# A transformer kernel on one Trainium2 core: first modulation as rows in column tiles, gate units in the first head's quarters, two reordered waits

## What is computed

```python
c_act = silu(c)
for i in range(2):                                   # first block
    mod = c_act @ ada_w[i] + ada_b[i]                # 1 x 2048 @ 2048 x 6144
    shift, scale, gate = split(mod, 3)
    h = rmsnorm(x, norm_g[i]) * (1 + scale) + shift
    y = retention(h) if i == 0 else latent_attention(h)
    x = x + gate * y
x = rmsnorm(x, final_norm_g)
# second block: forgetting + dilated attention, then the expert layer:
# per token 8 heads x 16 chosen of 16384 experts
hdn = gelu(sum(expert_down[e] * xn)); x += sum_e(gate_e * hdn_e * expert_up[e])
out = rmsnorm(x, final_norm_gain)
```

## Time and profile before

| | us |
|---|---|
| three runs | 2998.37, 3003.18, 3003.22 |
| median | 3003.18 |
| the profiled execution, its time | 2998.47 |
| the profiled execution, its span | 2996.7 |
| PE, DVE, ACT, POOL busy | 2888.4, 2077.0, 1113.0, 541.4 |
| moved by DMA | 799.62 MB, mean 267 GB/s |

### The profile page before, as it was taken

The page is one execution under the profiler, slowest core; times in us unless marked ns, Lnnn a source line. Parts: engine busy times, 40 slices in busy tenths (PEclk is TensorE's granted clock), DMA queues, the critical chain, the costliest instruction groups (busy, mean ns, idle before and its releaser), DMA issues.

```text
span 2996.7 us, 41682 instructions
## 1 busy us (share of the span) xinstructions
PE 2888.4 (96%) x16537; PEld 2414.1 (81%) x16537; DVE 2077.0 (69%) x3117; ACT 1113.0 (37%) x1729; POOL 541.4 (18%) x524
## 2 busy tenths in 40 slices
PE   7999999999999999999999999999999989999998
PEld 7999999998878977798987899888889977444443
DVE  5778777778775455754556658995568999666666
ACT  1344444444445444544445542012026977000000
POOL 0000000000000000000000002333446457544443
PEclk9899999999999999999999999999999999999999
DMA  9977777777866644466443545999998888999998
GB/s 329 355 236 266 267 265 267 268 264 259 295 212 188 173 117 136 147 182 186 126 123 127 192 157 194 338 323 402 395 345 287 292 290 302 404 409 409 409 409 325
DMA packets 359297, 799.62 MB, mean 267 GB/s; under 512 B 40152, under 2 KB 99920, under 8 KB 358336
## 3 DMA queue, kind: packets, MB, share of 16 engines
q1 hardware_dynamic: 284480, 506.28, 49.8%
q0 software_dynamic: 74624, 290.69, 26.3%
HBM read 794.76 MB, written 2.10 MB: 266 GB/s over the span
## 4 chain that ended last, share of the span: by engine, by line
PE 70%; DMA 15%; DVE 6%; issue 3%; ACT 3%; POOL 2%; SPq 0%; DVEq 0%; ACTq 0%; POOLq 0%
PE ps L2021 16%; PE ps L2023 15%; PE ps L2022 15%; PE ps L2570 13%; DMA s<-in_up_rows,s 12%; POOL s L717 2%; DVE s L1971 2%; DMA s<-in_down_rows,s 2%; PE ps L2065 1%; DVE s L1952 1%; PE ps L2601 1%; DVE r L1239 1%; PE ps L2645 1%; PE ps L2615 1%; PE ps L2303 1%
## 5 line engine op out<-in xcount | busy, mean ns | idle before, releaser
L2021 PE MATMUL ps<-r,r 128*128 128x256 f32 (+1 forms) x3232 | 1045.3, 323 | 7.1 <-DVE r L1239 5.3
L2023 PE MATMUL ps<-r,r 128*128 128x256 f32 (+1 forms) x3232 | 1027.2, 318 | 0.0
L2022 PE MATMUL ps<-r,r 128*128 128x256 f32 (+1 forms) x3232 | 1026.8, 318 | 0.0
L1239 DVE TENSOR_TENSOR r<-s,r 128x1024 fp32r<-128x1024 f32 (+2 forms) x532 | 640.2, 1211 | 432.3 <-ACT r L732 431.3
L732 ACT CAST r<-s 128x1024 fp32r<-128x1024 f32 (+2 forms) x532 | 548.9, 1039 | 786.5 <-PE ps L2023 721.4
L2021 PEld LDWEIGHTS ps<-r,r 128*128 128x128 f32 x3232 | 621.2, 192 | 57.6 <-issue 13.7
L2022 PEld LDWEIGHTS ps<-r,r 128*128 128x128 f32 x3232 | 621.2, 192 | 43.2 <-issue 5.3
L2023 PEld LDWEIGHTS ps<-r,r 128*128 128x128 f32 x3232 | 620.5, 192 | 40.5
L2696 PE MATMUL ps<-s,big 128*128 128x512 f32 x1024 | 443.2, 596 | 1.5 <-DMA s<-in_up_blocks 1.5
L1971 DVE SCALAR_TENSOR_TENSOR s<-s,s,s 128x1024 f32<-128x1024 f32 x256 | 328.4, 1283 | 165.4 <-DMA s<-in_up_rows,s 163.7
L1952 DVE CUSTOM_DVE_ANT_0 s<-s,s 128x1152 f32<-128x1152 f32 x256 | 345.6, 1352 | 111.7 <-DMA s<-in_down_rows,s 110.1
(11 more groups left out here) (300 smaller groups left out, 2468.6 us busy)
## 6 DMA issues: line engine op xcount, KB each, us to landing
s<-in_ada_w SPq DMA_DIRECT2D x192, 512.0 KB, 5.9
s<-in_ret_w_in SPq DMA_DIRECT2D x128, 512.0 KB, 5.4
s<-in_up_blocks SPq DMA_DIRECT2D x128, 512.0 KB
s<-in_down_blocks SPq DMA_DIRECT2D x128, 448.0 KB
s<-in_w_in SPq DMA_DIRECT2D x96, 512.0 KB, 3.9
s<-in_ret_w_in SPq DMA_DIRECT2D x128, 256.0 KB, 3.9
s<-in_ret_w_out SPq DMA_DIRECT2D x64, 512.0 KB, 5.7
s<-in_mla_w_in SPq DMA_DIRECT2D x48, 512.0 KB, 3.7
```

The costliest lines, as they stand in the source:

```text
L1239: v.tensor_tensor(lo_of(w), raw_of(w), hi_of(w).bitcast(F), ALU.subtract).then_inc(*lo_made.to(w))
L2021: pe.matmul(o, lh, rh, start=start, stop=False, skip_group_check=True)
L2022: pe.matmul(o, lh, rl, start=False, stop=False, skip_group_check=True)
L2023: return pe.matmul(o, ll, rh, start=False, stop=stop, skip_group_check=True)
```

## The change

1. **Modulation as rows.** `first_direct` and `first_sum` call `into_row`: the column of `cact` (or ones), broadcast to 32 columns, is the stationary operand, and the block's 1024 columns move in four pieces of 256, each into its own 32 partitions of bank 7 (four column tiles). ACT copies the 128 x 256 result to `MODROW`, PE transposes it (`first_turn`), and DVE reads every 32nd column as the modulation. `TENSOR_K` has 8 of 16 k's instead of 6.
2. **Layout of the inputs.** `ada_first` and `ret_first` hold the same numbers as the blocks of the first modulation and the 24 units of head 0, rearranged ahead of the launch so that each entry is one piece of 4 KB per partition (before: two of 2 KB, or four of 1 KB for q and k).
3. **Order of the first head.** Each quarter has six units: two `qk`, two `vals`, two `gate` (w = 6q to 6q + 5), with the sixteen blocks of the next quarter behind the first four. `scores(0)` moves ahead of the last two gate units. Normed x is transposed once, ahead of the modulation, and ACT copies it to `XNT0` in SBUF; scaling reads it there. DVE takes the norm ahead of its first block.
4. **Small loads.** The constant table and the nine gain and bias loads go from SP's queue to GpSimd's, behind x.
5. **Latent values.** The wait for the copy of the values moves from the scores of each group to their first reader.
6. **Ones.** The last one-hot of tile 0 is made after down row 251, the coefficients of tile 1 ahead of the first up row, and tile 1's one-hots ahead of up rows 1 to 32.

```diff
+        XNT0 = at(32 * KB, 16, 256)
+        MODROW = at(YG + 5376, 256)
...
         def mod_entry(q, k):
-                cols_ = A["ada_w"][0][k * 128:(k + 1) * 128, 0:2 * D].rearrange("p (s n) -> p s n", s=2)
-                return [(ap.rearrange("p (s n) -> p s n", s=2), cols_[:, :, q * 512:(q + 1) * 512])]
+            return ("mod", 1024, lambda ap: [(ap, A["ada_first"][q, k])], (q, k))
+        def first_unit(w):
+            return ("w", 1024, lambda ap: [(ap, A["ret_first"][w])], None)
...
         for q in range(4):
-                if q < 3:
-                    plan += [mod_entry(q + 1, 4 * i + k) for k in range(4)]
-        cols512(ret_in, 8192)
+            for x in range(6):
+                plan.append(first_unit(6 * q + x))
+                if q < 3 and x < 4:
+                    plan += [mod_entry(q + 1, 4 * x + k) for k in range(4)]
...
-        TENSOR_K = (1, 4, 7, 10, 13, 15)
+        TENSOR_K = (1, 3, 5, 7, 9, 11, 13, 15)
...
-        HOT_AT = [190 + 2 * q for q in range(29)] + [248, 250]
+        HOT_AT = [190 + 2 * q for q in range(29)] + [248, 250, 251]
...
         def scalar(s):
...
-            s.wait_ge(*col_b.at(0))
             s.activation(XN[:, 0, :], X[:, 0, :], ACT.Square, scale=float(D) ** -0.5, accum_out=st[:, 0:1]).then_inc(*sq_a.to("N0"))
...
+            for p in range(8):
+                s.wait_ge(*turned.at(("N0", p)))
+                s.copy(flat(XNT0[:, 2 * p:2 * p + 2, :]), bank_of_pair("N0", p)).then_inc(*xnt_made.to(p))
             for q in range(4):
-                cast(4 * q)
+                s.wait_ge(*summed.at(("first", q)))
+                if q:
+                    s.wait_ge(*mod_turned.at(q - 1))
+                s.copy(MODROW, bank[7][:, 0:256]).then_inc(*mod_copied.to(q))
+                cast(6 * q)
...
         def vector(v):
...
-            entries(4)
-            v.wait_ge(*cols.at("all"))
...
-            v.wait_ge(*col_b.at(0))
             v.tensor_tensor_reduce(XN[:, 1, :], X[:, 1, :], X[:, 1, :], 1.0 / D, 0.0, ALU.mult, ALU.add,
                                    st[:, 1:2]).then_inc(*sq_v.to("N0"))
+            norm("N0", 0)
             entries(9)
-            norm("N0", 0)
+            v.wait_ge(*cols.at("all"))
...
             hidden(1)
-            first_ones(0, 31)
+            coefficients(1)
             add_row(0)
-            coefficients(1)
-            add_row(1)
-            add_row(2)
-            for n in range(3, 256):
+            for n in range(1, 256):
+                if n <= 32:
+                    first_ones(1, n - 1)
                 add_row(n)
-                if n < 35:
-                    first_ones(1, n - 3)
...
         def tensor(pe):
...
+            def into_row(q, column, w, first, last):
+                for m in range(4):
+                    r = pe.matmul(bank[7][32 * m:32 * m + 32, 0:256], column.broadcast_to([128, 32]), w[:, m * 256:(m + 1) * 256],
+                                  start=first, stop=last, skip_group_check=True)
+                return r
...
-                for m in range(8):
-                    r = pe.matmul(bank[6 + q % 2][:, m:m + 1], raws[i % 8][:, m * 128:(m + 1) * 128], cact[:, k:k + 1],
-                                  start=k == TENSOR_K[0] and m == 0, stop=False, skip_group_check=True)
-                r.then_inc(*mod_t.to(i))
+                into_row(q, cact[:, k:k + 1], raws[i % 8], k == TENSOR_K[0], False).then_inc(*mod_t.to(i))
...
+            def first_turn(q):
+                take(6)
+                pe.wait_ge(*mod_copied.at(q))
+                for j in range(2):
+                    r = pe.transpose(bank[6][:, j * 128:(j + 1) * 128], MODROW[:, j * 128:(j + 1) * 128], IDN)
+                r.then_inc(*mod_turned.to(q))
...
-            for k in TENSOR_K[1:]:
+            for k in TENSOR_K[2:5]:
+                first_direct(0, k)
+            for p in range(8):
+                turn("N0", p, XN, normed("N0"))
+            for k in TENSOR_K[5:]:
                 first_direct(0, k)
             first_sum(0)
+            first_turn(0)
             for q in range(4):
+                for x, (f, u) in enumerate((f, u) for f in (qk, vals, gate) for u in (2 * q, 2 * q + 1)):
+                    if q < 3:
+                        for k in TENSOR_K:
+                            if k // 4 == x:
+                                first_direct(q + 1, k)
+                        if x == 4:
+                            first_sum(q + 1)
+                    if q == 3 and x == 4:
+                        scores(0)
+                    f(0, u, 6 * q + x)
+                    if q < 3 and x == 4:
+                        first_turn(q + 1)
...
-                        pe.wait_ge(*vm_copied.at((g, 1)))
...
                     pe.wait_ge(*flip_copied.at(("M", h)))
+                    if h % 4 == 0:
+                        pe.wait_ge(*vm_copied.at((h // 4, 1)))
```

More of the change, by code:

```diff
@@ L810, in scalar @@
                     turn("N0", p, gs, mod[:, 0:16], HT)
-                for x in range(1, 4):
-                    cast(4 * q + x)
-            for x, dst in enumerate((cosR, sinR, cosM, sinM)):
-                s.wait_ge(*angle.at(x))
-                s.activation(dst, RQ[x], ACT.Sin).then_inc(*sines.to(x))
+                for x in range(1, 6):
+                    cast(6 * q + x)
+                    if q == 3 and x == 3:
+                        for a, dst in enumerate((cosR, sinR, cosM, sinM)):
+                            s.wait_ge(*angle.at(a))
+                            s.activation(dst, RQ[a], ACT.Sin).then_inc(*sines.to(a))
             def v_copy(h):
-                w = 15 if h == 0 else 24 * h + 15
+                w = 21 if h == 0 else 24 * h + 15
                 if h == 0:
@@ L1436, in vector @@
             for q in range(4):
-                entries(entry_of[4 * q] + 1 + (2 if q < 3 else 0))
+                entries(entry_of[6 * q])
                 first_modulation(q)
@@ L1500, in vector @@
             qk_rotate(0)
-            for w in range(16, 20):
+            for w in (20, 21):
                 step(w)
             decay(0)
-            for w in range(20, 24):
+            for w in (22, 23):
                 step(w)
@@ L2103, in turn @@
                 r.then_inc(*turned.to((x, p)))
-                free[b] = turn_a.at((x, p)) if p % 2 else turn_v.at((x, p))
+                free[b] = xnt_made.at(p) if x == "N0" else turn_a.at((x, p)) if p % 2 else turn_v.at((x, p))
             def normed(x):
@@ L2736 @@
     every["table"], every["decay"] = table, decay
+    first = every["ada_w"][0][:, 0:2 * D].reshape(16, 128, 2, 4, 512)
+    every["ada_first"] = np.ascontiguousarray(first.transpose(3, 0, 1, 2, 4)).reshape(4, 16, 128, 1024)
+    ret = every["ret_w_in"][0]
+    heads = [np.concatenate([ret[:, 0:256], ret[:, 2048:2304]], axis=1), ret[:, 4096:4608], ret[:, 8192:8704]]
+    every["ret_first"] = np.ascontiguousarray(np.stack(
+        [f[u * 256:(u + 1) * 256].reshape(2, 128, 512).transpose(1, 0, 2) for q in range(4) for f in heads
+         for u in (2 * q, 2 * q + 1)])).reshape(24, 128, 1024)
     rows = every.pop("peer_down_2")[0]
```

110 lines of the change are left out of this document (44 added, 66 removed).

## The result

The changed kernel took 2965.75 us (median of four runs, 2959.61 to 2967.84), the kernel before 3003.2 beside it (median of four, 2998.37 to 3005.46): a ratio of 0.9873 [0.9859, 0.9888], 37.5 us less. The forecast was 2970 (2957 to 2992). The profiled execution is the shortest of its runs, 2959.61 us with a span of 2957.8; against the profiled execution of before (2998.47) it is 38.9 us shorter.

The account below looks back on a forecast made before the run. PE was taken as the bound, with DMA also at its limit early and in the expert stage's last 440 us. 2998.5 - 22 - 7 - 1.5 = 2968.0, plus half of 4.7, gave 2970 us, range 2957 to 2992.

Parts of the forecast that it names:

- The row product: First head's modulation on PE: four column tiles run side by side, so a block takes 0.7 us.
- The landing of the last block: First head: the last modulation block lands at 120.2 us instead of 127.8.
- The packets: First head's transfers: 4 KB pieces raise DMA from 379 to 409 GB/s, -8.1 us, bounds 0 and -8.1.
- From the landing to `values`: First head's end: nine units, last block with sum and turn, scores and waits take 32.4 us.
- Part 1: First head: `values` begins at 152.6 instead of 174.2, -22 us, bounds -9 and -27.
- The latent wait: Latent heads: PE's four stops of 8.1 us before the groups' first scores go; -7 us, bounds -3 and -9.
- The ones: Expert stage: tile 1's loop starts about 5 us earlier, but DMA must bring the rest; -1.5 us, bounds 0 and -5.
- the point of the part: First head's quarters: six units in the time of four, DMA the bound, PE idle some 5 us in each.
- Rival A: First head: tiles run one behind the other, block 1.9 us, Part 1 gives nothing; 2992 us, chance 0.09.
- Rival C: First head: rows one behind the other at a clock of 0.845, `values` 21 us later; 3013 us, chance 0.05.
- rival B: First head: packets bring no more than 379 GB/s and the start gains nothing; 2983 us, chance 0.10.
- (D): Whole kernel: all bounds on the good side, -27, -9 and -5; 2957.5 us, no chance of its own given.

Follow-up runs that it names:

- experiment 4: Changed kernel with each row product as four full-array matmuls, one behind the other, into the same 256 columns: 2970.12 us, ratio 0.989.
- experiment 3: Changed kernel with the first modulation's blocks and head 0's units read in their old layout, pieces of 2 KB and 1 KB: 2972.25 us, ratio 0.9894.
- experiment 7: Changed kernel with ten of a quarter's 16 blocks on PE instead of eight: 2971.35 us, ratio 0.9889.
- 11: Changed kernel with ten of 16 blocks on PE and a needless matmul ahead of blocks 3, 7, 10 and 15 of quarters 1 to 3: 2963.07 us.
- control: The changed kernel once more, with no edit: 2966.97 us, ratio 0.9875.
- experiment 1: Kernel before, with only the wait for the latent values moved to their first reader: 2988.15 us beside 3004.05, ratio 0.9945.
- 2: Kernel before, with only the last one-hot of tile 0 and tile 1's coefficients and one-hots moved as in the change: 3003.2 us beside 3004.05.
- experiment 6: Changed kernel with the table and the nine small loads back on SP's queue between entries 5 and 6: 2963.85 us, ratio 0.986.

## Why the prediction was right, step by step

**The row product (0.7 us side by side).** Right: 0.64. The four tiles run beside each other, their starts 6 to 8 ns apart (215 ns on the full array); serially the same eight records take 1.89, a factor of 2.95. The Trainium skill, TensorE: Matmul & The Clock Gate, Part 3, lists 2.38 for three column tiles; this trace agrees in kind for four tiles of fp32. Of a drain at a mode change, which the Trainium skill, TensorEngine Tiling (Array Packing), Key Properties, warns of, the trace shows little. Here nothing is waited for ahead of the row product:

```profile
124.42 0.39 PE L2021 MATMUL ps<-r,r 128*128 128x512 f32 x1
124.65 0.39 PE L2022 MATMUL ps<-r,r 128*128 128x512 f32 x1
124.97 0.64 PE L2060 MATMUL ps<-s,s 128*32 128x256 f32 x8
125.53 0.39 PE L2020 MATMUL ps<-r,r 128*128 128x256 f32 x1
```

Full-array matmuls of 512 columns start 0.23 us apart, the row product 0.32 behind the last of them: about 0.09 us. The idle times of 0.15 to 0.26 us ahead of other blocks end with a transfer by the profile, and experiment 4, which never changes the mode, has one of 0.23.

**The landing of the last block (120.2).** Right: 121.45, with two errors that cancel. The first unit starts 8 us earlier (41.3; the sum had given the start 5). The packets carry most of their term: experiment 3 puts it at 5.3 to 6.5 us of the whole time, where the sum had 8.1. But the quarters take 31 to 32 us, not 28.2. DMA has its 409 GB/s only outside the slow windows. What SP's queue waits for in the first 160 us of after (total, times, longest):

```profile
SPq L656 <- DVE r L1244: 57.8, 26, 5.9
SPq L656 <- DVE s L1257: 25.2, 25, 2.1
```

SP stands most of the time before a buffer that DVE has not yet freed by a low part; the six windows from 60 to 120 us average 390 GB/s, by which 22 entries of 0.524 MB are 29.6 us. The remaining 1.4 us or so of a quarter I could not place. Experiments 7 and 11 speak against DVE's products as the cause; DVE's order, the stand before the turned modulation, is what lengthens SP's waits at the change of quarters.

**From the landing to `values` (32.4).** Right: 121.45 to 152.74 is 31.3. Part 1 together: 21.5 in the profiles against -22. That 152.6 was forecast and 152.7 measured is luck in the tenths: the landing's errors cancel, and the profiled execution is the one without a fall of the clock. What the sum lacked is that this part varies from one execution to the next. I had taken the unit at 2.96 us throughout and left the clock only as a thing that could prove me wrong; the control shows windows at 0.66 to 0.74 and 7 us more. Experiments 1 and 2, with the first head of before, have `values` at 177.6 and 177.8, the profile of before 174.2, so a part of the 4.7 us between before's profile and its median is the same thing.

**The latent wait (-7, bounds -3 and -9).** The mechanism was right and the size was off by half: 12.6 us in this stage of the profiles, 13.9 in experiment 1, 15.9 in its timed runs, all outside the bounds. The mis-sized term is the price of a stop: I counted what PE stood still (8.1 us) and not the matmuls behind it, which over 1050 to 1180 us lost 6.5 us by a mean clock of 0.95.

**The ones (-1.5, bounds 0 and -5).** The stage gives 1.5 in the profiles, but the timed runs give 0.85 and -0.2 us of gain with either first head: nothing measurable, the bound of 0. The step "the DMA must still bring the rest" held; the 1.1 us that the earlier start should repay is under what can be told here.

**Small loads, order, rivals.** The small loads' move costs nothing (experiment 6), as the zero in the sum had it. The gate units in the quarters carry 7.1 us; that was "the point of the part". Rival A's price was wrong: serial rows cost 3 to 4.5 us over control and not 22. I had tied its first unit to 49.3 us (measured 42.4) and given it quarters of 35.2 us (33 to 35), so that `values` came 12.6 us too late; and the kernel that it is measured against loses some us to its clock, which the forecast did not. Rival C (slower) was built from the same terms, with a clock of 0.845; experiment 4 has the opposite, a clock of 1.00, so its price of 43 us over the forecast has no support. Of rival B the half that says that packets bring nothing was run, with the start's gain left in: 2972.25, where B as a whole had 2983.

**The total.** 2998.5 less 38.9 in the profiles, against 30.5 in the sum; the difference of 8.4 us is the latent stage (5.6) and gains of 1.5 and 1.8 us between the next block's turns and the up rows, which the sum had at nothing and no experiment took apart, less 0.5 in the first head. Taken one by one, the latent wait (15.9), the gate units (7.1), the packets (5.3), the tiles (3.2), the small loads and the ones (nothing) come to 31.5 us of the 37.5; the norm and the turns of x ahead of the modulation were not taken back, and what is left is theirs or the scatter's. Between the medians it is 37.5 us, as the result's median lies 6 us over its profile and before's 4.7 over its own. The forecast was 4 us high for the median, inside the range; the case that I had as (D), all bounds good, lies 8 us on the other side.

## What to carry to other kernels

Price a stop of TensorE by the stop and by what runs behind it: look at the granted clock of the windows after it, and count the units there at their 1.2 GHz duration. Where a wait of about 2 us can't be removed, a needless matmul ahead of it is a cheap try; here the granted clock of every run was higher in both kernels that had it, and the medians 5.8 and 8.3 us lower, the first with runs that overlap and the second across two chips. Look also for what stands behind the slowed engine in program order: here DVE's place before the turned modulation passed a slow unit on to the weight queue. And when several streams of a small product can stand in column tiles, the gain is mostly what else the freed time lets in: here the serial form lost 3 to 4.5 us, while the gate units in that time were worth 7 and the 4 KB pieces 5 to 6.

## What the runs showed of the hardware that I had not expected

- One and the same kernel falls to 1.2 GHz or not behind stops of nearly equal length: 1.92 and 2.01 us, and even 2.87, kept the clock at 1.00 in one execution, 1.92 and 2.11 us did not in another. The execution decides, not only the code.
- A fall of PE's clock can show up a window later as a drop of the DMA rate (404 then 245 GB/s in control, 408 then 230 in experiment 7), where DVE stands before PE's result (3.58 us instead of 0.66) with the ring's next low part queued behind. Where it does not, the rate stays (409 and 410 GB/s behind control's falls at 80 and 110 us).
- An fp32 row product on the whole array, 1.89 us instead of 0.64, made the kernel only 3 to 4.5 us slower than control, and its granted clock was 1.00 in every window from 20 to 160 us.
- One piece of 4 KB per partition moves 403 to 416 GB/s where pieces of 2 KB and 1 KB move 379 to 390, both with the DMA engines at their full share.
